# First block's feed-forward of layer two by seven quarter products, conditioning sums all in layer one

## What is computed

```
FFN_HIDDEN = 2816
# first block, layer i in 0, 1 (after its attention/convolution/state-space mixer)
h = rmsnorm(x, norm_ffn[i])
gt, up = jnp.split(h @ w_ffn_in[i], 2, axis=-1)
x = x + (jax.nn.silu(gt) * up) @ w_ffn_out[i]
# second block: the conditioning
cs = jax.nn.silu(c)
mod = (cs @ w_ada[l] + b_ada[l])[:, None, :]      # 1024 x 6144 weights, one row
```

## Time and profile before

| | us |
|---|---|
| median of 3 runs | 2596.02 |
| range of the runs | 2595.3 to 2596.52 |
| the profiled execution | 2594.88 |
| its span, first to last instruction | 2593.4 |
| PE busy in the span | 2527.2 (97%) |
| DVE busy | 1534.6 (59%) |
| POOL busy | 1232.0 (48%) |
| ACT busy | 951.3 (37%) |

### The profile page before, as it was taken

The page is one execution under the profiler, slowest core; times in us unless marked ns, Lnnn a source line. Parts: engine busy times, 40 slices in busy tenths (PEclk is TensorE's granted clock), DMA queues, the critical chain, the costliest instruction groups (busy, mean ns, idle before and its releaser), DMA issues. The chain is left out here.

```text
span 2593.4 us, 33178 instructions
## 1 busy us (share of the span) xinstructions
PE 2527.2 (97%) x13084; PEld 2022.5 (78%) x13084; DVE 1534.6 (59%) x1870; ACT 951.3 (37%) x1349; POOL 1232.0 (48%) x891
## 2 busy tenths in 40 slices
PE   7999999999999999999999999989999999899997
PEld 6887778788887778777878888768777777688886
DVE  8984435843333787443484333479865477766665
ACT  5332543322222533344332222334335563433332
POOL 4434345444444533443545444447893234565551
PEclk9999999999999999999999999989999999899998
DMA  5222223254333412322234433232232122133321
GB/s 177 82 66 82 78 75 96 90 163 129 117 117 123 132 58 66 92 76 82 90 129 140 129 121 122 90 120 90 74 97 66 58 98 66 57 115 96 108 82 65
DMA packets 226636, 253.57 MB, mean 98 GB/s; under 512 B 9152, under 2 KB 202944, under 8 KB 226240
## 3 DMA queue, kind: packets, MB, share of 16 engines
q1 hardware_dynamic: 226176, 251.12, 31.3%
q10 hardware_dynamic: 320, 0.52, 0.1%
HBM read 246.90 MB, written 4.19 MB: 97 GB/s over the span
## 5 line engine op out<-in xcount | busy, mean ns | idle before, releaser
L221 POOL TENSOR_TENSOR sb_w_lo<-sb_raw,sb_w_hi 128x512 fp32r<-128x512 f32 x684 | 915.7, 1366 | 1045.8 <-ACT sb_w_hi L214 1043.8
L243 PE MATMUL ps<-sb_a_hi,sb_w_hi 128*128 128x512 f32 x1472 | 600.8, 408 | 21.7 <-DVE sb_w_lo L221 9.1
L244 PE MATMUL ps<-sb_a_lo,sb_w_hi 128*128 128x512 f32 x1472 | 582.9, 396 | 0.0
L245 PE MATMUL ps<-sb_a_hi,sb_w_lo 128*128 128x512 f32 x1472 | 582.6, 396 | 0.0
L214 ACT ACTIVATE sb_w_hi<-sb_raw 128x1024 fp32r<-128x1024 f32 x344 | 360.8, 1057 | 490.6 <-PE ps L245 425.9
L243 PEld LDWEIGHTS ps<-sb_a_hi,sb_w_hi 128*128 128x128 f32 x1472 | 277.0, 188 | 120.3 <-issue 36.8
L245 PEld LDWEIGHTS ps<-sb_a_hi,sb_w_lo 128*128 128x128 f32 x1472 | 276.9, 188 | 67.9
L244 PEld LDWEIGHTS ps<-sb_a_lo,sb_w_hi 128*128 128x128 f32 x1472 | 277.6, 189 | 63.9 <-issue 2.6
L243 PE MATMUL ps<-sb_b_hi,sb_w_hi 128*128 128x512 f32 x736 | 293.4, 399 | 11.4 <-DVE sb_b_lo L3085 7.4
L244 PE MATMUL ps<-sb_b_lo,sb_w_hi 128*128 128x512 f32 x736 | 291.8, 397 | 0.0
L245 PE MATMUL ps<-sb_b_hi,sb_w_lo 128*128 128x512 f32 x736 | 291.3, 396 | 0.0
(11 more groups left out here) (469 smaller groups left out, 4097.9 us busy)
## 6 DMA issues: line engine op xcount, KB each, us to landing
sb_raw<-in_w_in_dram SPq DMA_DIRECT2D x148, 512.0 KB, 3.7
sb_raw<-in_w_ffn_in_dram SPq DMA_DIRECT2D x88, 512.0 KB, 5.1
sb_ada<-in_w_ada_dram SPq DMA_DIRECT2D x48, 512.0 KB, 4.5
sb_raw<-in_w_ffn_out_dram SPq DMA_DIRECT2D x44, 512.0 KB, 3.9
sb_raw<-in_w_ff_dram SPq DMA_DIRECT2D x32, 512.0 KB, 4.2
sb_f_raw_d<-in_w_ff_dram SPq DMA_DIRECT2D x32, 512.0 KB, 3.8
sb_raw<-in_w_mix_o_dram SPq DMA_DIRECT2D x16, 512.0 KB, 3.5
sb_raw<-in_w_conv_o_dram SPq DMA_DIRECT2D x8, 512.0 KB, 3.4
```

Source lines behind the costliest of these rows:

```text
L221: ins = pool.tensor_tensor(w_lo[:, s, here], raw[:, s, here], w_hi[:, s, here].bitcast(F32), ALU.subtract)
L243: pe.matmul(out, wh, hi, start=first and i == 0, stop=False)
L244: pe.matmul(out, wh, lo, start=False, stop=False)
L245: ins = pe.matmul(out, wl, hi, start=False, stop=last and i == len(rhs) - 1)
```

## The change

`ffn1` becomes two functions. `ffn1_first`, for layer one, is the old one with all of the conditioning: the blocks are 512 columns wide (`ADA_W`), still 12 of them, two loads of 1 MB each, and three transposed parts in place of two. `ffn1_last`, for layer two, has none of it, and from chunk 2 on it computes the up product with seven quarter products. K and the tokens are halved; the two halves of the weights' columns are the gate's and the up's. A round r (of 9) has nine pieces in the order M1 M4 M2 D0 M6 M5 M7 D1 M3: the seven products of chunk r+2 and the two down pieces of chunk r+1; the last round has M3 before D1. A piece fills one of the four slots, as a unit did. The two down tiles of the last chunk follow as two further pieces. Everything is written out, there is no loop.

```diff
-ADA_BLOCKS = 6 * 1024 // 256 // DEPTH
+ADA_W = 512
+ADA_BLOCKS = 6 * 1024 // ADA_W
...
-                                src = d["w_ada2"][512 * k:512 * k + 512, bass.ds(l * (256 * ADA_BLOCKS) + block * 256, 256)]
+                                src = d["w_ada2"][512 * k:512 * k + 512, bass.ds(block * ADA_W, ADA_W)]
...
-                                for b in range(ADA_BLOCKS // 2):
+                                for b in range(ADA_BLOCKS):
...
+        def ffn1_last(l, loaded, rounded, following):
...
+                        for r in range(mixes):
+                            load_down(2 * r + 2)
+                            sp.wait_ge(s_made, 4 * r + 4)
+                            sp.wait_ge(lo_pool, products * r + lo_of[M6])
+                            if r + 1 < mixes:
+                                load_pair(r + 1, 1)
+                            sp.wait_ge(lo_pool, products * r + lo_of[M7])
+                            if r + 1 < mixes:
+                                load_pair(r + 1, 0)
+                            load_down(2 * r + 3)
...
+                        for r in range(mixes):
+                            for j in (M1, M4, M2, M6, M5, M7, M3):
...
+                                for q in range(2):
+                                    ins = pool.tensor_tensor(by_tile(w_lo[:, s, at]), source[j][:, 4 * q:4 * q + 4, :],
+                                                             by_tile(w_hi[:, s, at].bitcast(F32)), ALU.subtract)
+                                if j == M2:
+                                    rest_down(piece(r, D0), 2 * r)
+                                if j == (M3 if r == mixes - 1 else M7):
+                                    rest_down(piece(r, D1), 2 * r + 1)
...
+                            down(piece(r, D0), r + 1, 2 * r, True, True)
...
+                        pe.wait_ge(hid_lo_done, 2 * mixes + 2)
+                        pe.wait_ge(up_free, 2 * mixes + 2)
+                        down(tail, chunks - 1, 2 * mixes, True, True, first_bank=0)
+                        down(tail + 1, chunks - 1, 2 * mixes + 1, False, True, tile_done=down_tile)
...
+                        act.wait_ge(t_made, 4)
+                        for k in (1, 0):
+                            act.activation(t_hi[:, 4 * k:4 * k + 4, :], t_all[:, 4 * k:4 * k + 4, :], ACT.Copy).then_inc(t_round, 1)
+                        round_unit(act, 8)
+                        round_unit(act, 9)
+                        round_to(2)
+                        hidden(1)
+                        for r in range(mixes):
+                            round_to(pieces * r + 4)
+                            act.wait_ge(piece_used, pieces * r + 1)
+                            act.activation(m1, ps[:, 0, :], ACT.Copy).then_inc(m1_kept, 1)
+                            round_to(pieces * r + 11)
+                            gate_part(r, slice(0, 3), C21)
+                            hidden_part(r, slice(0, 3), 2 * r + 3)
+                            round_to(pieces * r + 13)
+                            gate_part(r, slice(3, 4), C12)
+                            hidden_part(r, slice(3, 4), 2 * r + 4)
```

More of the change, by code:

```diff
@@ L1433, in mixer1, with ffn1_first @@
                 phase_end(mixer_sems)
-        def ffn1(l, loaded, rounded, following):
+        def ffn1_first(l, loaded, rounded, following):
             chunks, ups, per = CHUNKS1, 4, 6
@@ L1601, in _ @@
                             go_up(last, last_u + n, 0, n)
-                        pe.wait_ge(ada_kept, 2)
+                        pe.wait_ge(ada_kept, 3)
                         for at, part in enumerate(of_parts):
-                            rows = 128 if at == 0 else 64
                             for m in range(NB):
-                                c = 16 * at + rows // 32 * m
-                                ins = pe.matmul(ps[:, 6, c:c + rows // 32], part[:, m * P:(m + 1) * P],
-                                                ident[0:rows, 0:rows:32], start=True, stop=True)
+                                c = 16 * at + NB * m
+                                ins = pe.matmul(ps[:, 7, c:c + NB], part[:, m * P:(m + 1) * P], ident[:, 0:P:32],
+                                                start=True, stop=True)
                         ins.then_inc(ada_full, 1)
@@ L1648, in chunk @@
                             hidden(c, parity)
-                        def both_squares(tiles):
-                            for kt in tiles:
-                                if kt < 4:
-                                    act.wait_ge(down_free, 2 * last - 1)
-                                else:
-                                    act.wait_ge(tile_added, kt - 3)
-                                act.activation(a_hi_32[:, kt, :], x[:, kt, :], ACT.Square).then_inc(next_square, 1)
-                                act.activation(a_lo_32[:, kt, :], x[:, kt, :], ACT.Square, scale=norm_gains[:, 0, kt:kt + 1])\
-                                    .then_inc(next_square, 1)
                         act_keep_row(act, row[:, :])
@@ L1687, in _ @@
                             round_unit(act, n)
-                        if mixes:
-                            act_next(act, range(4), next_gain, a_hi, [b_hi_32[:, kt, :] for kt in range(4)], lambda kt: act.wait_ge(down_free, 2 * last - 1))
-                        else:
-                            both_squares(range(4))
+                        act_next(act, range(4), next_gain, a_hi, [b_hi_32[:, kt, :] for kt in range(4)], lambda kt: act.wait_ge(down_free, 2 * last - 1))
                         round_unit(act, total + 2)
-                        if not mixes:
-                            both_squares(range(4, KD))
                     @block.vector
@@ L1709, in add_ada @@
                         def add_ada(block):
-                            out = ada_sums[:, bass.ds(block * 256, 256)]
+                            out = ada_sums[:, bass.ds(block * ADA_W, ADA_W)]
                             for kt in range(KD):
@@ L1781, in _ @@
                         dve.wait_ge(ada_full, 1)
-                        for at, n in ((0, 16), (16, 8)):
-                            there = l * (2 * ADA_BLOCKS) + at
-                            dst, b, src = mod[:, there:there + n], b_ada[:, at:at + n], ps[:, 6, at:at + n]
-                            (step if at == 0 else Count(dve, mod_read)).done(
+                        for at in (0, 16, 32):
+                            dst, b, src = mod[:, at:at + 16], b_ada[:, at:at + 16], ps[:, 7, at:at + 16]
+                            (Count(dve, mod_read) if at == 32 else step).done(
                                 tt(dst.rearrange("p (g m) -> p g m", m=NB), src.rearrange("p (m g) -> p g m", m=NB),
@@ L1789, in _ @@
                         df.done(tt(x[:, 0:4, :], x[:, 0:4, :], ps[:, 0:4, :], ALU.add))
-                        if mixes:
-                            dve_next(dve, step, range(4), next_gain, a_hi, a_lo, [b_hi_32[:, kt, :] for kt in range(4)])
-                        else:
-                            def add_squares(kt):
-                                for n, sums in enumerate((a_hi_32, a_lo_32)):
-                                    dve.wait_ge(next_square, 2 * kt + n + 1)
-                                    step.done(tt(sums[:, 0, :], sums[:, 0, :], sums[:, kt, :], ALU.add))
-                            for kt in range(1, 4):
-                                add_squares(kt)
-                            for kt in range(4, KD):
-                                if kt < KD - 1:
-                                    dve.wait_ge(down_tile, kt - 3)
-                                else:
-                                    multiplied(dve, total - 1)
-                                Count(dve, tile_added, kt - 4).done(
-                                    tt(x[:, kt, :], x[:, kt, :], ps[:, LAST_DOWN_BANK + kt - 4, :], ALU.add))
-                                if kt > 4:
-                                    add_squares(kt - 1)
-                            add_squares(KD - 1)
@@ L3113, in build @@
                 parts, part_kept) = in_ffn
-            ffn1(l, SLOTS, AHEAD, (lambda n: first_of_mixer1(l + 1, n)) if l + 1 < DEPTH else first_of_mixer2)
-            before[0] += units_f1
+            if l + 1 < DEPTH:
+                ffn1_first(l, SLOTS, AHEAD, lambda n: first_of_mixer1(l + 1, n))
+                before[0] += units_f1
+            else:
+                before[0] += ffn1_last(l, SLOTS, AHEAD, first_of_mixer2)
             (
```

436 lines of the change are left out of this document (419 added, 17 removed).

## The result

The changed kernel takes 2602.57 us (median of 20 runs, 2598.91 to 2606.16), the kernel before, timed beside it, 2597.34 (20 runs, 2594.52 to 2601.75). The ratio is 1.0018, 95% interval 1.0011 to 1.0024: slower by 5 us, at the edge of what was called "the same". The forecast was 2599.5. It was right in sign and lies 3 us low; 1.3 us of that is the kernel before itself, whose median beside it is 2597.34 and was 2596.02 when the forecast was made.

A forecast was written before the change was run, and what follows sets the result against it. PE, busy 97%, was taken to set the pace. Layer two -11.8 and layer one +15.3 sum to +3.5 on the profiled 2594.9, 2598.4; the median lies 1.1 higher, 2599.5 us. Range 2585 to 2611.

The forecast's parts named there:

- layer one, head: Start of layer one's feed-forward: wider conditioning blocks and their loads delay u4 and u10, +7 us (+3 to +10).
- stop ahead of the sums: Layer one's tail: PE stops while the last wide conditioning block is loaded and computed, +4.5 us (+2.5 to +5.5).
- sums, transposes and clock: Layer one's tail: 24 sum passes for 12 and 24 transposes for 16, +2.8 us; low clock after the stop, +1.
- eight rounds: Layer two: eight round intervals of 30.8 us against 33.65, -22.4 us, with +1 for rounds in which POOL is late.
- chunks 0 and 1, first round: Layer two's beginning: a 1.1 us wait goes, but u8, M4, M2 and D0 come late, +3.5 us (0 to +6).
- end, with the clock: Layer two's end: PE waits 6 us on the last chunk's hidden channels, +5.1 us; low clock after it, +1.
- POOL's capacity: Layer two's rounds: POOL's 18 remainder instructions take 26.3 to 30.1 us, barely fitting in PE's 30.8.
- The first rival: Layer two: POOL's round is the bound, waiting on M7's pair load; each interval 1.2 us longer, +9, 2608; chance 0.26.
- The fourth rival: Layer one's head: POOL and DVE fully exclude each other, wide block 16.3 us, +3, 2602.5; chance 0.08.
- The second: Rival: shorter waits at both layers' ends, no clock fall in layer one's tail, -9 to -10 us, 2587; chance 0.24.
- the third: Rival: all the delays at the layers' ends hide, -22 us, 2574; chance 0.04.
- The likeliest case: The forecast itself, whole kernel: 2599.5 us, within 2594 to 2605; chance 0.38.

The follow-up runs named there:

- tanh_first: Changed kernel with ACT taking the tanh of the three mixed banks before rounding the next round's M1 and M4, last round unchanged: 2599.26 us, 1.0012 of the kernel before.
- loads_later: Changed kernel with layer one's conditioning loads set behind the second unit load of their chunk in SP's list: 2595.96 us, 0.9996 of the kernel before.
- tail_round: Changed kernel with ACT, in the last round, rounding the second last down piece behind the last hidden channels: 2596.3 us, 0.9991 of the kernel before.
- loads_halves: The changed kernel with conditioning loads set later in SP's list, plus its buffer given back in halves: 2590.61 us, 0.9978 of the kernel before.

## Why the prediction came out right, step by step

| step | forecast | trace |
|---|---|---|
| layer one, head | +7 | +5.4 |
| stop ahead of the sums | +4.5 | +4.8 |
| sums, transposes and clock | +2.8 + 1 | +4.15 |
| layer one | +15.3 | +14.3 |
| eight rounds | -22.4 + 1 | -22.4 + 3.6 |
| chunks 0 and 1, first round | +3.5 | +1.0 |
| end, with the clock | +5.1 + 1 | +7.4 |
| layer two | -11.8 | -10.3 |
| up to the second block | +3.5 | +4.05 |
| medians | +3.5 (2599.5) | +5.2 (2602.57) |

The sum is nearer than its parts. The rounds lost 2.6 us more than was allowed and the end of layer two 1.3 more; its beginning lost 2.5 less and the head of layer one 1.6 less. That these made up for one another to half a microsecond is luck; what was foreseen are the places and causes of the losses, the rounds' apart.

**The rounds' own time** was right: tanh_first runs them in 30.89, the forecast had 30.8. **POOL's capacity** too: it is not the bound, and by more than the forecast thought. In a round of the changed kernel its 18 instructions take 24 us, where 26 to 30 were named, and it stands idle for 7 to 8, 4.9 or more of them ahead of M6. The first rival's price rested on these too large numbers.

**Lateness in the rounds** was sized too small, 1 for 3.6. The first rival had the right load, that of M7's pair, and the wrong way from it to PE. It followed it through M1's remainder, where there is room; it goes through ACT's list to the tanh. The same fault in the last round had been seen in the prediction and priced. It was not looked for in the other eight. The waits that the profile names there come to 1.2 us of the 3.6.

**The beginning of layer two** was sized too large, +3.5 for +1.0. The waits at M4 and D0 of round 0 are there (0.6 and 1.1), but u8 cost 0.3 and not 1, and the 1.1 ahead went as said.

**The end of layer two** was right in mechanism: the load landed 4.0 us after its issue, the tanh began at M3's start + 6.8, the hidden remainder ended at + 14.9, in the forecast's 14 to 15.5. The stop was 6.4 for 6, and the clock took 1.8 and not 1 (nine multiplications 0.43 us apart, not 0.23).

**The head of layer one** came out at 5.4 for 7. u4's rounding came 4.1 later, as forecast (4.4): SP issued its load 2.0 later (487.75 for 485.71), and the rest went by in the load itself. (A megabyte at 300 to 400 GB/s is 2.6 to 3.5 us, not 2.5 to 3.) But PE had some slack in front of it and waited 2.6. Two waits of 0.6 and 0.7 on h's remainders are add_ada(0)'s 2 us. The second block took 12.4 us (forecast 12.5 to 13.5), and u10 cost 1.0 and not 2.6. loads_later confirms the cause, the unit loads behind the conditioning's in SP's list.

**The rule of the port pair.** Beside POOL's remainders a 128x512 three-operand instruction of DVE takes 10.97 / 7 = 1.57 us in the row above, and POOL's own take 6.61 / 4 = 1.65 there, where the two alone take 0.75 and 1.28, in sum 2.03. The Trainium skill, "SBUF — State Buffer", section "SBUF: two separate sides", has the port pair as an exclusive lock for a whole instruction, by which a pair would take the sum. The trace agrees in that both slow each other down, and not in the size. The fourth rival, by which the block would have taken 16.3 us, is out: it took 12.4.

**The tail of layer one** was right in each part: the stop (4.8 for 4.5), and the sums, transposes and clock (4.15 for 3.8).

**The medians** lie 1.1 further apart than the shifts up to the second block. I put that down to the granted clock at the later seams; no run isolates it.

**Rivals.** The second, short waits at the ends, and the third fell on the same rows. The likeliest case was the one that happened. The chance for slower (0.35) was somewhat low: 2602.57 is above the 2601.2 that was named, though against the kernel before as timed beside it, 2597.34, it stands just at the 0.2%.

## What to carry to other kernels

A saving on the bounding engine is an upper limit. Before it is counted, go through the ends of the stage, list by list, and ask of each engine what stands ahead of the instruction on which the critical chain depends. Here a rounding that waits for a load ahead of a tanh cost 4 us in one round and 3 in eight others, loads behind a wait in SP's list cost another 4, and a buffer given back only whole another 5 or more. No work was added, only its place was bad. Mending the one round, SP's list and the buffer turned +5 into -16; with those in place, the eight rounds gave 0.6 us more in the medians, which is not clear of the spread. When a fault of order is found in one place, look for it wherever the same lines are repeated.

## What the runs showed of the hardware

Stops of PE of 2.0 us (tail_round) and 4.8 and 6.4 us (changed kernel) were followed by 3 to 5 us at the 1.2 GHz level, while one of 1.1 us (loads_halves) was not. But one and the same stop of 2.43 us in the second block was followed by some 6 us at the low clock in the changed kernel's profile, and by none in that of the kernel before. So in these traces a short stop cost its length and, in some executions and not in others, up to some 3 us more. Clock and time went together roughly over the changed kernel's runs: 0.987 at 2599.55 us, 0.983 at 2606.16, but 0.985 at 2598.91.

That a wide instruction costs less than twice a narrow one was expected, but beside POOL it costs relatively less still: 128x256 takes 0.52 alone and 1.30 beside POOL, 128x512 0.78 (5.48 / 7 at the head) and 1.57. In these rows POOL's presence adds 0.8 us to an instruction of either width.
